# Two transformer blocks on one core: memory keys and values computed side by side, first loads from one queue

## The reference, cut to what matters

```python
hm = rms_norm(mem, g_mem[layer])
xk = (hm @ w_xk[layer]).reshape(b, m_len, X_HEADS, X_HEAD_DIM)   # 2048 -> 512
xv = (hm @ w_xv[layer]).reshape(b, m_len, X_HEADS, X_HEAD_DIM)   # 2048 -> 512
...
h = rms_norm(x, g_mix[layer])
proj = h @ w_in[layer]
```

## Time and profile before

| | before |
|---|---|
| median of 3 runs | 2405.24 us (2405.1 to 2406.16) |
| profiled execution, its own time | 2405.57 us |
| its span in the trace | 2403.8 us |
| TensorE busy | 2390.6 us |
| VectorE, ScalarE busy | 1698.0 us, 1134.3 us |

### The profile page before, as it was taken

The page is one execution under the profiler, slowest core; times in us unless marked ns, Lnnn a source line. Parts: engine busy times, 40 slices in busy tenths (PEclk is TensorE's granted clock), DMA queues, the critical chain, the costliest instruction groups (busy, mean ns, idle before and its releaser), DMA issues.

```text
span 2403.8 us, 31556 instructions
## 1 busy us (share of the span) xinstructions
PE 2390.6 (99%) x10880; PEld 1992.1 (83%) x10880; DVE 1698.0 (71%) x2276; ACT 1134.3 (47%) x1526; POOL 10.4 (0%) x23
## 2 busy tenths in 40 slices
PE   8999999999999999999999999999999999999999
PEld 7988888888888888888888888888888888888887
DVE  7778777675567756668897977767556765667875
ACT  7454545644344434445544445454444443444553
POOL 0000000000000000000000000000000000000000
PEclk9999999999999999999999999999999999999999
DMA  8645555555565665655556564565656565565654
GB/s 314 217 167 182 167 166 169 193 189 196 193 194 188 198 194 184 204 186 187 182 192 201 179 219 158 193 202 183 201 193 194 182 205 193 191 196 177 208 187 165
DMA packets 126282, 461.96 MB, mean 192 GB/s; under 512 B 14032, under 2 KB 14416, under 8 KB 125408
## 3 DMA queue, kind: packets, MB, share of 16 engines
q1 hardware_dynamic: 123360, 446.22, 56.5%
q0 software_dynamic: 2384, 13.68, 1.6%
q10 hardware_dynamic: 432, 0.59, 0.1%
HBM read 458.35 MB, written 2.10 MB: 192 GB/s over the span
## 4 chain that ended last, share of the span: by engine, by line
PE 95%; DVE 4%; ACT 0%; DMA 0%; issue 0%; ACTq 0%; DVEq 0%
PE acc L455 90%; DVE w_lo L1289 1%; PE acc L644 1%; DVE heads L1424 1%; PE acc L707 1%; PE acc L460 1%; PE pt L535 1%; PE po L690 1%; PE po L682 1%; PE pt L661 0%; DMA raw<-stream 0%; PE acc L496 0%; PE acc L628 0%; DVE tmp_c L1912 0%; DVE tmp_a L1409 0%; DVE tmp_a L1413 0%
## 5 line engine op out<-in xcount | busy, mean ns | idle before, releaser
L1289 DVE TENSOR_TENSOR w_lo<-raw,w_hi 128x1024 fp32r<-128x1024 f32 x844 | 1023.8, 1224 | 597.1 <-ACT w_hi L857 584.8
L857 ACT ACTIVATE w_hi<-raw 128x1024 fp32r<-128x1024 f32 x843 | 890.4, 1060 | 1080.7 <-PE acc L455 970.0
L455 PE MATMUL acc<-w_hi,norm_hi 128*128 128x512 f32 (+1 forms) x2232 | 869.4, 390 | 0.0
L455 PE MATMUL acc<-w_hi,norm_lo 128*128 128x512 f32 (+1 forms) x2232 | 865.6, 388 | 0.0
L455 PE MATMUL acc<-w_lo,norm_hi 128*128 128x512 f32 (+1 forms) x2232 | 594.3, 388 | 0.1
L455 PEld LDWEIGHTS acc<-w_lo,norm_hi 128*128 128x128 f32 x2232 | 417.6, 188 | 87.3 <-DVE w_lo L1289 1.8
L455 PEld LDWEIGHTS acc<-w_hi,norm_lo 128*128 128x128 f32 x2232 | 419.2, 188 | 85.1
L455 PEld LDWEIGHTS acc<-w_hi,norm_hi 128*128 128x128 f32 x2232 | 419.1, 188 | 84.9
L455 PE MATMUL acc<-w_hi,mix_hi 128*128 128x512 f32 x1088 | 426.3, 392 | 2.6 <-ACT w_hi L1102 1.4
L455 PE MATMUL acc<-w_hi,mix_lo 128*128 128x512 f32 x1088 | 424.7, 390 | 0.0
L455 PE MATMUL acc<-w_lo,mix_hi 128*128 128x512 f32 x1088 | 291.6, 390 | 0.0
(11 more groups left out here) (220 smaller groups left out, 910.0 us busy)
## 6 DMA issues: line engine op xcount, KB each, us to landing
raw<-stream SPq DMA_DIRECT2D x843, 512.0 KB, 3.9
x<-x_tok POOLq DMA_DIRECT2D x2, 2048.0 KB, 9.8
heads<-x_in POOLq DMA_DIRECT2D x4, 512.0 KB, 7.8
x<-mem_tok POOLq DMA_DIRECT2D x2, 1024.0 KB, 7.1
heads<-rows_in POOLq DMA_DIRECT2D x2, 1024.0 KB, 9.0
heads<-decay_in POOLq DMA_DIRECT2D x4, 512.0 KB, 5.3
heads<-mem_in SPq DMA_DIRECT2D x3, 512.0 KB, 10.2
out<-x SPq DMA_DIRECT2D x3, 512.0 KB, 5.7
```

What stands on the lines that cost most here:

```text
L455: last = pe.matmul(acc[:, slot, c * NB:c * NB + width], a[:, k * T + c * P:k * T + (c + 1) * P], w[:, s, kk * width:(kk + 1) * width], sta ...
L857: act.activation(w_hi[:, (units.fixed - 1) % RING, :], src, ACT.Copy).then_inc(w_hi_ready, 1)
L1289: dve.tensor_tensor(w_lo[:, s, :], src, w_hi[:, s, :].bitcast(F32), ALU.subtract)\
```

## The change

The host interleaves the units of the two weights: key unit 0, value unit 0, key unit 1, and so on. TensorE works them in this order, with the keys in the first accumulator and the values in the second (`part=range(ki, ki + 1)`, `back` for the accumulator before). So the keys end with unit 14 and the values with unit 15. SyncE alone issues the loads of unit 0, between the memory parts; memory parts 4 and 5 go out after the ring's loads 5 and 7. ScalarE and VectorE prepare the memory parts later, and VectorE takes the keys after its split of unit 17 and the values after its split of unit 18.

```diff
@@ sync
-            for i in range(3):
-                load_mem(i)
+            first_unit = stream[0:1].rearrange("o p n -> (o p) n")
+            load_mem(0)
+            sp.dma_start(raw[:, 0, 0:NB], first_unit[:, 0:NB]).then_inc(first_half_landed, 16)
+            load_mem(1)
+            sp.dma_start(raw[:, 0, NB:], first_unit[:, NB:]).then_inc(raw_landed[0], 16)
             load(1, 1)
+            load_mem(2)
+            load(2, 2)
+            load(3, 3)
             load_mem(3)
-            for r in range(2, RING):
-                load(r, r)
-            load_mem(4)
-            load_mem(5)
-            with sp.Fori(0, UNITS // RING - 1) as i:
+            for r in range(RING, 2 * RING):
+                sp.wait_ge(raw_read, r - RING + 1)
+                load(r, r - RING)
+                if r % 2:
+                    load_mem(4 + (r - RING) // 2)
+            with sp.Fori(1, UNITS // RING - 1) as i:
@@ tensor
-            one_block(NU, mix, token_major=True, need=lambda ki: (operand_ready, ki + 2 if ki < 2 else ki // 2 + 3),
-                      halves=True)
-            one_block(NU, mix, token_major=True)
+            def memory_need(ki):
+                return operand_ready, ki + 2 if ki < 2 else ki // 2 + 3
+
+            for ki in range(NU):
+                one_block(NU, mix, token_major=True, need=memory_need, part=range(ki, ki + 1), back=int(ki > 0),
+                          halves=True)
+                one_block(NU, mix, token_major=True, part=range(ki, ki + 1))
@@ scalar
             act.dma_start(vec[:, 0:VN], vectors).then_inc(vec_landed, 16)
-            first_unit = stream[0:1].rearrange("o p n -> (o p) n")
-            act.dma_start(raw[:, 0, 0:NB], first_unit[:, 0:NB]).then_inc(first_half_landed, 16)
-            act.dma_start(raw[:, 0, NB:], first_unit[:, NB:]).then_inc(raw_landed[0], 16)
...
-            for i, n in enumerate((1, 2, 1, 1)):
+            split(1)
+            for i, n in enumerate((2, 2, 1)):
                 mem_hi(2 + i)
                 split(n)
-            split(1)
             wait_rows()
             act.activation(lam[:, 2:4], lam[:, 2:4], ACT.Exp).then_inc(func_ready, 1)
             split(2)
+            mem_hi(5)
             wait_rows()
@@ vector
-            for i, n in enumerate((0, 1, 1, 2, 1, 1)):
+            for i, n in enumerate((0, 2, 2, 2)):
                 mem_low(i)
                 split(n)
...
             split(1)
+            mem_low(4)
...
             split(1)
+            mem_low(5)
             dve.wait_ge(func_ready, funcs.add())
...
-            split(2)
-            take_plain(NU, chunks(heads, XK))
-            split(1)
+            split(3)
             for b in range(NBD):
                 split(1)
                 x_low(b)
-            split(3)
-            take_plain(NU, chunks(heads, XV))
+            split(2)
+            take_plain(2 * NU - 1, chunks(heads, XK))
+            split(1)
+            take_plain(1, chunks(heads, XV))
             split(4)
@@ host
-    parts = [weight_units(a["w_xk"][0]), weight_units(a["w_xv"][0]),
+    memory = np.stack([weight_units(a["w_xk"][0]), weight_units(a["w_xv"][0])], axis=1).reshape(-1, P, UE)
+    parts = [memory,
```

## The result

| | median | runs | before, same chip | ratio, 95% interval |
|---|---|---|---|---|
| the change | 2413.21 us | 7, 2412.42 to 2414.18 | 2405.11 us | 1.0033 (1.0024 to 1.0042) |

The change costs 8.1 us by the medians; the interval times 2405 gives 5.8 to 10.1. I had forecast 2408.4, a loss of 3.2 us (within 0.2%), and a range that ended at 2413.0. The sign was right, the forecast loss less than half of the measured one, and the result lies just outside the range. The profiled execution has a span of 2410.7 against 2403.8 us, 6.9 more. Its parts can be followed to the end.

What follows compares the result with a forecast made beforehand. TensorE was taken to bound the kernel, through its pauses and clock. Start -2.4, stall +4.3 and clock +1.3 summed to +3.2 us, giving a median of 2408.4 us, range 2402.8 to 2413.0.

Steps and rivals of the forecast that it cites:

- What bounds: TensorE, busy 2390.6 of 2403.8 us: only its standing or lower clock counts; all gain lies in the first 15 us.
- Start: Units 0 and 1: second half of unit 0 lands near 5.9 instead of 8.45, -2.4 us (-1.3 to -2.9).
- rival C: First loads: one queue moves no faster, second half still lands near 8; +5.2 us, 2410.4; chance 0.10.
- Side by side costs nothing: Interleaved units: same number of matmuls, copies and subtractions, memory preparation hides, x_in near 18 harmless; cost nothing.
- Stall: Before unit 18 TensorE stands for T - 4.0, as ScalarE's squares wait for x_tok: +4.3 us (2.1 to 7.2).
- T: Time to landing of the 2048 KB x_tok, issued after the keys are taken: 8.3 us, bounds 6.1 and 11.2.
- Clock: After the pause before unit 18 TensorE may restart at 1.2 GHz: +1.3 us (0 to 2.6), the middle.
- the sum of +3.2: Whole kernel: -2.4 at the start, +4.3 stall and +1.3 clock give a loss of 3.2 us.
- rival B: Before unit 18 x_tok takes 11.2 us, with clock 2.6: +7.4 us, 2412.6; chance 0.13.

Runs made afterwards that it cites:

- gain_rows later: The changed kernel with the small broadcast transfer gain_rows moved from right behind x_tok to 87 us later: 2412.72 us, ratio 1.0032 to the kernel before.
- one queue alone: The kernel before with only the first transfers issued by SyncE in order of need, keys first, then values: 2404.30 us, ratio 0.9996.
- side by side alone: The changed kernel with first loads as before, x_tok issued at ten units and keys taken right after the split of unit 15: 2405.10 us, ratio 0.9998.

## Why the prediction was wrong

- **What bounds.** Right: nothing but TensorE's pauses and its clock counted. Unit 24 is already shifted by as much as the marker, to within 0.01 us, in all ten kernels, so behind the first 24 units nothing was gained or lost up to there, as forecast.
- **Start, -2.4 (-1.3 to -2.9).** The range was right; the exact hit is in part luck. The profiled change gives -2.44. The second half took 4.4 us to land (issued 2.14, so 6.5, forecast 5.9) against 6.8, the block started at 7.22 (forecast 7.1), a gain of 1.93. The other 0.5 is the clock, which rose 4.3 us after that start and not 5.25, and the last section shows how much this varies. Seven traces with these loads in the side-by-side kernels have -1.6 to -2.6. "The loads gain nothing", rival C, falls.
- **Side by side costs nothing.** Right for the work and the memory operands, as far as the traces show. x_in went out at 21.64, not 18, and cost nothing either.
- **Stall, T - 4.0 with T = 8.3, +4.3.** The mechanism was right: the instruction, the engine, the unit, and what stands behind it. The size was off: 6.87. This is the step that failed, and it has two halves. It makes up 2.6 of the 3.8 us by which the profiled pair (+6.98) lies above the sum of +3.2; the clock makes up the other 1.25. T measured 10.1, +1.8. And the issue came 0.8 later than I had it: taken back to times of before it stood at 51.76 + 2.44 = 54.20 against 53.4. I had let VectorE's splits follow ScalarE's copies at once; but VectorE carried four low parts of x between its splits and was itself the slower, with the split of unit 17 ending at 50.3 instead of 49.0.
- **Why T was wrong.** I took the one sample from 232 us and called it nearest. The same transfer at that place took 8.0 to 9.9 us over all eleven traces, of which 8.3 is near the lowest, and the first one 9.1 to 11.6 (at 52 to 53 us, in four of them, 9.1, 9.9, 10.1 and 11.6). The reason I gave (fewer neighbours than at 35.84) was argued and not shown. The middle of the two rows I had, 9.8, would have been better.
- **Clock, +1.3 (0 to 2.6).** Measured 2.55, the upper end, which my own rows had priced at 2.6. Taking the middle of two cases that exclude each other gave a figure that no trace shows: the price was 1.6 to 2.55 us in five kernels, and at most 0.14 in the two with a pause under 1 us. The rule of the Trainium skill that stood beside it ("TensorE: Matmul & The Clock Gate", "Why this matters for your kernels") says that a long idle gap between matmuls returns the clock to half rate; here the trace agrees, with a granted clock of 0.50 behind the pause.
- **The range and the rivals.** With T = 10.1, the later issue and the whole clock the sum is -2.4 + 6.9 + 2.6 = +7.1, which rival B had at +7.4. I gave it 0.13. The list of rivals has no case with a T between the two rows, which gives nearly as much once a long pause brings the whole clock price with it. The medians lie 8.1 apart, 1.1 more than the profiled pair. The profiled execution before took 0.5 us more than its median and that of the change 0.6 less; that start and T vary (above) could account for this, but it was not traced.
- **What I missed.** The take of the keys. I had its move in the list and priced it only as a trigger. That it also guards unit 16, with 1.2 us to spare (53.10 against 54.34), stands in my own numbers. In the profiled change the take ended at 51.46 and unit 16 started at 51.90, so only 0.44 was left and it had no price. In the trace of "gain_rows later", the same kernel up to there, it did: unit 16 started 0.49 us late, behind the take. And it is why moving x_tok alone gives back only about half of the loss.

## What to carry to other kernels

When a result is finished later, list all that its semaphore releases: here one copy both started a 2 MB transfer and freed an accumulator, and each needed its own place. A large transfer needs a slot where neither its own reader nor the stream beside it is close to late; price its time to landing by the spread over all its instances, with the clock's price added as soon as a pause of some 3 us or more is likely, as in the cases below. An order by need on one queue moved the urgent transfer up by 1.9 us in the change, and it paid only as far as nothing later gave it back.

## What the runs showed that was not expected

- The clock after a pause: pauses of 0.85 and 0.94 us left it at 2.4 GHz. Those of 3.0, 3.2, 4.9, 5.9 and 6.7 us each put it down to 1.2 GHz, at a cost of 1.6, 1.6, 2.2, 2.3 and 2.55 us. So the two pauses of about 3 us cost half as much again as their length. Each of these is one traced execution; no run has a pause between 0.94 and 3.0 us.
- The clock at the start does not follow the start of the work at a fixed distance. The second block began at 9.15, 7.83 and 7.22 (before, one queue alone, the change), and full rate came 5.3, 6.1 and 4.3 us later. With side by side alone the block began at 9.15 again, and full rate came at the latest 3.5 us later, since its matmuls from 12.68 on are 0.23 us apart. I had assumed 5.25. The kernel with gain_rows later and the one with one queue alone began that block at 7.78 and 7.83, and unit 2 at 13.87 and 15.37: 1.5 us apart by the clock alone.
- The stretches show a granted clock of 1.00 before 10 us, where the starts of the matmuls give 1.2 GHz; after the later pauses they show the fall. At the start of a program the starts of the matmuls are the safer reading.
